# Three groups of gate products per token tile instead of four in a two-layer hybrid trunk kernel

## The chip, the cores and the metric

The kernel runs on one core of a Trainium2 chip. The metric is the device time of one execution in microseconds (us); lower is better.

## The reference

The reference is a trunk of two layers over 1024 tokens of width 1024, in float32. Each layer projects its input, runs four token mixers (forgetting attention, retention, the gated recurrence `hgrn2`, attention on a memory), merges them through per-channel sigmoid gates, and goes through a grouped mixture of experts. Two parts matter here: the recurrence over chunks of 64 tokens, and the gated merge of the four branches.

```python
# gated recurrence, one chunk (q, k, v, log f); b = cumsum(log f)
a = einsum('bhik,bhjk,bhijk->bhij', qn, kn, decay)
o = einsum('bhij,bhjv->bhiv', a, vn) + einsum('bhik,bhkv->bhiv', qn * exp(b), state)
new_state = exp(b_last)[..., None] * state + einsum('bhjk,bhjv->bhkv', kn * exp(b_last - b), vn)
o = o * rsqrt(mean(o * o) + eps) * norm_g * silu(g)
...
# gated merge
up = einsum('bsnc,ncd->bsnd', branches, w_branch[l])
gates = sigmoid(gate.reshape(B, S, 4, 1024))      # gate = x @ w_in[l][:, gate columns]
mixed = sum(gates * up, axis=2) @ w_out[l]
```

## The kernel before

**Numbers.** Every float32 operand of a big product is held as two float16 parts, a high and a low one, and one product is three matmuls (high by high, high by low, low by high) of 128x128 by 128x512. ScalarE (ACT) makes the high part of a chunk of weights (`high_parts`, L785), and VectorE (DVE) the low part from it (`low_parts`, with `low_part` at L1274).

**Units and groups.** The gate columns of the four branches are cut into 16 units of 256 columns; unit `u` is one load of weights into one of two slots. A unit has four groups `g` (two blocks of 128 columns by two halves of 512 tokens), so a layer has 64 groups. `gate(g)` gives the place of the group: `place = g // 16`, which branch is merged, in `ORDER = (0, 1, 3, 2)`; the recurrence's branch is last. In its plain form a group (`gate_group`) is 8 products for the gate into a bank of PA and 2 products for the branch into a bank of PB: 30 matmuls, 120 for the unit. ACT takes the tanh (`gate_tanh`, L979), DVE multiplies (`gate_mul`, L1536), and from place 1 on adds to the running sum as well (L1539).

**The seven-product form.** For the last units of a layer (`sev_group`) the gate product of a unit, seen as 2x2 blocks (input half by column block by token half), is made with seven block products in place of eight. A block product is 4 products, 12 matmuls; the 24 matmuls of the branches stay. This takes sums of weight blocks (`sums_1_3`, `sum_2`, `sum_4`) and sums of blocks of the input (`x_sum_full`, `x_sum_high`, `x_sum_low`; eight pieces per layer). `PLAIN = 9` units are plain and `SEV = 7` are in the seven-product form; `SEV_G = 4 * PLAIN` is the first group of these.

**The order of the work.** It is written out by hand, one program per engine, and every engine runs its own in order. The plain groups are interleaved with the recurrence, tile by tile (128 tokens, `NT = 8`): two groups ahead (`PRE = 2`), four in each tile `t` (`g = PRE + 4 * t` to `g + 3`), two behind the loop, then the seven-product units. In tile `t` TensorE (PE) runs:

1. six transposes into PC (L2418), group `g`, the state product, the running sums of tile `t + 1` into PC, group `g + 1`;
2. the scores (L2441), group `g + 2`, the outputs (L2449, L2454; they post `h_o`);
3. two transposes of the finished output of tile `t - 1` into PC (L2218, `transpose_o`), group `g + 3`.

After `h_o` ACT squares the output (L1096), DVE reduces it (L1689), GpSimd takes the power (L687), and DVE finishes the row into `ON` (L1695 to L1699, posts `h_on`). The two transposed blocks of tile `t - 1` are copied out of PC by ACT (`copy_ot`, L898) and DVE (`low_ot`, L1274 as OT<-PC,OT), which posts `ot_cp`; on DVE `low_ot` stands behind the reduction. The next tile's transposes write the same PSUM tile PC and begin with these waits:

```python
pe.wait_ge(h_pr, at(h_pr, t + 1))
pe.wait_ge(ot_cp, at(ot_cp, 3 * NT + max(t, 1)))
```

With the count as it is posted, the second one waits in tile `t` (from 2 on) for the copy of exactly the blocks that tile `t - 1` transposed in its step 3. In tiles 3, 5 and 7 DVE also makes two pieces of the input sums (L1593 to L1597 and the low part at L1274), and ACT their high parts (L1010).

**Splitting the next unit's weights.** `next_unit_high(g)` and `next_unit_low(g)` stand behind the tanh and the multiplication of group `g`. Which chunks they split depends on `g % 4` alone:

```python
return (range(0), range(0, 3), range(3, 5), range(0))[g % 4]
```

The third of the three chunks at remainder 1 can be made by ACT only when DVE has taken the first.

Of the kernel before, what the change touches and what calls it, by code (L numbers as in the profile page):

```python
# [30 lines left out]
NT = T // P  # L31
# [56 lines left out]
PRE = 2  # L88
ORDER = (0, 1, 3, 2)


PLAIN = 9
SEV_U, SEV_G, SEV = GATE_U + PLAIN, 4 * PLAIN, GATES - PLAIN
RAW = 5
B11, T1, T3, B22, B21, T2, T4, BRANCH = range(8)
# [4 lines left out]
def chunks_to(u):  # L100
    return 8 * min(u, GATE_U) + 5 * min(max(u - GATE_U, 0), PLAIN) + 8 * max(u - SEV_U, 0)

# [19 lines left out]
def trunk(nc, x, mem, w_in, b_in, w_mem_kv, hgrn_lb, hgrn_norm_g, w_branch, w_out, ln_g, ln_b,  # L122
          w_router, b_router, w_e_in, w_e_out, consts, chunk_mask, out):
    with ExitStack() as ctx:
# [315 lines left out]
        def gate(g):  # L440
            u, i = GATE_U + g // 4, g % 4
            c, half = (i // 2, i % 2) if g < SEV_G else QUARTERS[i]
            return u, g // 16, ORDER[g // 16], g // 4 % 4 * 2 + c, c, half
# [329 lines left out]
        def _(act):  # L773
# [58 lines left out]
            with act.Fori(0, LAYERS) as l:  # L832
# [142 lines left out]
                def gate_tanh(g):  # L975
                    u, place, n, d, c, half = gate(g)
                    act.wait_ge(g_z, at(g_z, g + 1))
                    act.wait_ge(g_mul, at(g_mul, g + 1))
                    nc.scalar.activation(TH[g % 2], PA[:, g % 2, :], ACT.Tanh,  # L979
                                         bias=bT[:, 6 + n * KD + d:7 + n * KD + d], scale=0.5 * UN).then_inc(g_sig, 1)  # L980
                    if place == NBR - 1:
                        act.wait_ge(mix_f, at(mix_f, g - 48 + 1))
                        nc.scalar.activation(MIXS[:, d, half, 0, :], MIXF, ACT.Copy, scale=0.5 * UN * SX
                                             ).then_inc(mix_hi, 1)
# [15 lines left out]
                def next_unit_high(g):  # L1000

                    u = GATE_U + g // 4 + 1
                    if u == SEV_U:
                        sev_high(u, (range(0), range(0, 2), range(2, 5), range(5, 8))[g % 4])
                    elif g < SEV_G:
                        high_parts(at, u, next_chunks(g))
# [70 lines left out]
                gate_tanh(1)  # L1077
                next_unit_high(1)
                for t in range(NT):
                    g = PRE + 4 * t  # L1080
                    act.wait_ge(h_tr, at(h_tr, t + 1))
                    nc.scalar.copy(WK[:, 1024:1792], flat(PC, 768)).then_inc(h_tc, 1)
                    if t + 1 < NT:
                        lf_high(t + 1)
                    gate_tanh(g)
                    next_unit_high(g)
                    if t + 1 < NT:
                        decays(t + 1)
                    gate_tanh(g + 1)
                    next_unit_high(g + 1)  # L1090
                    if t in (3, 5, 7):
                        x_sum_high(t // 2 - 1, 0)
                    gate_tanh(g + 2)
                    next_unit_high(g + 2)
                    act.wait_ge(h_o, at(h_o, t + 1))
                    nc.scalar.activation(paired(WK[:, 2560:2816]), by_bank(PD, HD, P), ACT.Square).then_inc(h_sq, 1)  # L1096
                    if t in (3, 5, 7):
                        x_sum_high(t // 2 - 1, 1)
                    if t >= 1:
                        copy_ot(3 * NT + t - 1, 2, t - 1)  # L1100
                    gate_tanh(g + 3)
                    next_unit_high(g + 3)
                for g in range(PRE + 4 * NT, SEV_G):
                    if g == PRE + 4 * NT + 1:
                        copy_ot(4 * NT - 1, 2, NT - 1)
                    gate_tanh(g)
                    next_unit_high(g)
# [154 lines left out]
        def _(v):  # L1262
# [51 lines left out]
            with v.Fori(0, LAYERS) as l:  # L1314
# [215 lines left out]
                def gate_mul(g):  # L1530
                    u, place, n, d, c, half = gate(g)
                    v.wait_ge(g_sig, at(g_sig, g + 3))
                    v.wait_ge(g_mm, at(g_mm, g + 1))
                    acc, up = MIX[:, d, half, :], PB[:, g % 2, :]
                    ups = UPS0 if place == NBR - 1 else UPS[g % 2]
                    stt(acc if place == 0 else ups, TH[g % 2] if g < SEV_G else TH7[g % 4], 1.0, up, ALU.add, ALU.mult).then_inc(g_mul, 1)  # L1536
                    v.drain()
                    if place in (1, 2):
                        tt(acc, acc, ups, ALU.add)  # L1539
                    if place == NBR - 1:  # L1540
                        tt(MIXF7[g % 2], acc, ups, ALU.add).then_inc(mix_f, 1)
# [111 lines left out]
                next_unit_low(1)  # L1653
                for t in range(NT):
                    a, b = t % 2, (t + 1) % 2
                    g = PRE + 4 * t
                    if t + 1 < NT:
                        lf_low(t + 1)
                    gate_mul(g)
                    next_unit_low(g)  # L1660

                    v.wait_ge(h_kv, at(h_kv, t + 1))
                    v.sem_inc(passed, 1)
                    kv = PD[:, :, 0:2 * HD].rearrange("p c (j d) -> p c j d", j=2)
                    tt(hstate[:, a, 1, :, :], hstate[:, a, 0, :, :], over(hdec[:, t % 2, :, 0], HD), ALU.mult)
                    v.drain()
                    tt(hstate[:, a, 1, :, :], hstate[:, a, 1, :, :], kv[:, 0, :, :], ALU.add)
                    v.drain()
                    tt(hstate[:, b, 0, :, :], hstate[:, a, 1, :, :], over(hdec[:, t % 2, :, 1], HD), ALU.mult)
                    v.drain()  # L1670
                    tt(hstate[:, b, 0, :, :], hstate[:, b, 0, :, :], kv[:, 1, :, :], ALU.add).then_inc(h_st, 1)
                    if t + 1 < NT:
                        decayed(t + 1)
                    if t in (3, 5, 7):
                        x_sum_full(t // 2 - 1, 0)
                    gate_mul(g + 1)
                    next_unit_low(g + 1)
                    v.wait_ge(h_a, at(h_a, t + 1))
                    v.sem_inc(passed, 1)
                    nc.vector.copy_predicated(paired(AT),  # L1680
                                              hmask[:, :].unsqueeze(1).unsqueeze(1).to_broadcast([P, 2, 2, P]),
                                              by_bank(PD, P, P)).then_inc(h_am, 1)
                    if t in (3, 5, 7):
                        x_sum_low(t // 2 - 1, 0)
                        x_sum_full(t // 2 - 1, 1)
                    gate_mul(g + 2)
                    next_unit_low(g + 2)
                    v.wait_ge(h_sq, at(h_sq, t + 1))
                    nc.vector.tensor_reduce(st[:, 4:8], heads(SQH), AX.X, ALU.add)  # L1689
                    v.drain()  # L1690
                    ts(st[:, 4:8], st[:, 4:8], 1.0 / HD, GN_EPS, ALU.mult, ALU.add).then_inc(h_var, 1)  # L1691
                    if t >= 1:
                        low_ot(3 * NT + t - 1, 2, t - 1)
                    v.wait_ge(h_rstd, at(h_rstd, t + 1))
                    tt(paired(N1), by_bank(PD, HD, P), over4(st[:, 8:12]), ALU.mult)  # L1695
                    v.drain()
                    tt(heads(N1), heads(N1), ngain[:, :].unsqueeze(1).to_broadcast([P, H, HD]), ALU.mult)
                    v.drain()
                    tt(ON[:, t % 2, :], N1, HN[:, t, 3 * BW:4 * BW], ALU.mult).then_inc(h_on, 1)  # L1699
                    gate_mul(g + 3)  # L1700
                    next_unit_low(g + 3)
                    if t in (3, 5, 7):
                        x_sum_low(t // 2 - 1, 1)
                for g in range(PRE + 4 * NT, SEV_G):
                    if g == PRE + 4 * NT + 1:
                        low_ot(4 * NT - 1, 2, NT - 1)
                    gate_mul(g)
                    next_unit_low(g)
                    if g == PRE + 4 * NT:
                        x_sum_full(3, 0)  # L1710
                x_sum_low(3, 0)
                x_sum_full(3, 1)
# [298 lines left out]
        def _(pe):  # L2011
# [72 lines left out]
            with pe.Fori(0, LAYERS) as l:  # L2084
# [324 lines left out]
                gate_group(1)  # L2409
                for t in range(NT):  # L2410
                    val = HN[:, t, BW:2 * BW]
                    g = PRE + 4 * t
                    pe.wait_ge(h_pr, at(h_pr, t + 1))

                    pe.wait_ge(ot_cp, at(ot_cp, 3 * NT + max(t, 1)))
# [42 lines left out]
                    if t >= 1:  # L2458
                        if t + 1 < NT:
                            pe.wait_ge(h_e, at(h_e, t + 2))  # L2460
                        transpose_o(3 * NT + t - 1, ON[:, (t - 1) % 2, :], 2)
                    gate_group(g + 3)
                for g in range(PRE + 4 * NT, SEV_G):
                    if g == PRE + 4 * NT + 1:
                        pe.wait_ge(h_on, at(h_on, NT))
                        transpose_o(4 * NT - 1, ON[:, (NT - 1) % 2, :], 2)
                    gate_group(g)
# [266 lines left out]
```

## Time and profile before

| what | value |
|---|---|
| time before, median of 3 runs | 2755.81 us (2753.03 to 2756.02) |
| the profiled execution's own time | 2761.64 us |
| its span | 2760.0 us |
| TensorE busy | 2571.6 us, 93% of the span |
| VectorE busy | 1672.1 us, 61% |
| ScalarE busy | 1215.6 us, 44% |
| mean granted TensorE clock | 0.966 of 2.4 GHz |

The span runs from the first to the last instruction; the own time lies 1.6 us above it, and the median 5.8 us below the own time. In the profile a time stamp is in microseconds from the start of the span, "L2332" is a line of the kernel, and an idle time is followed by what ended it. A matmul of 128x512 is recorded with 0.38 us, but the starts of two in a row lie 0.216 us apart, since they overlap; it is the distance of starts that counts in a sum.

### The profile page before, as it was taken

What the parts mean: (1) busy time and instruction counts of PE and PEld (TensorE: products, weight loads), DVE (VectorE), ACT (ScalarE), POOL (GpSimd) and SP (SyncE); (2) the same over time, 40 slices, a digit from 0 to 9 for tenths busy, and PEclk for the clock granted to TensorE, in tenths of its full rate; (3) what the DMA queues carried; (4) which work ended last, traced back from release to release, by engine and by line L of the source; (5) the groups of instructions that cost most, each with busy time, mean ns of one, the idle gap of its engine ahead of it and who ended that gap; (6) DMA issues with size and microseconds to landing.
All of it is one profiled execution on the core that took longest, in us unless ns stands there. A gap on an engine that the chain in (4) does not pass through costs nothing.

```text
span 2760.0 us, 55929 instructions
## 1 busy us (share of the span) xinstructions
PE 2571.6 (93%) x20734; PEld 1588.2 (58%) x20735; DVE 1672.1 (61%) x2735; ACT 1215.6 (44%) x1978; POOL 336.1 (12%) x242
## 2 busy tenths in 40 slices
PE   7999999999999869999979999999999997699993
PEld 5555555554444458888645565555544444688882
DVE  4244574566666658875643455745666666687884
ACT  4245423232343137765642454233323431376774
POOL 0000000000000013443320000000000000144443
PEclk9999999999999979999979999999999998899996
DMA  7210001111115459998843000011111154599996
GB/s 287 78 61 1 32 20 55 42 39 45 51 58 205 153 197 346 363 355 269 250 157 108 32 1 32 21 57 39 39 58 53 53 196 171 196 354 356 362 337 182
DMA packets 153278, 394.15 MB, mean 143 GB/s; under 512 B 14284, under 2 KB 63864, under 8 KB 151872
## 3 DMA queue, kind: packets, MB, share of 16 engines
q1 hardware_dynamic: 135936, 339.09, 34.0%
q0 software_dynamic: 16544, 46.00, 6.8%
q10 hardware_dynamic: 608, 6.55, 0.6%
q8 instruction: 116, 1.90, 0.3%
q14 instruction: 74, 0.61, 0.1%
HBM read 342.41 MB, written 53.38 MB: 143 GB/s over the span
## 4 chain that ended last, share of the span: by engine, by line
PE 80%; issue 5%; DVE 5%; DMA 3%; PEld 3%; ACT 2%; DVEq 1%; SPq 0%; PEldq 0%; POOL 0%; ACTq 0%; POOLq 0%
PE PA L2567 12%; PE PA L2021 7%; PE PA L2022 7%; PE PA L2023 7%; PE PD L2575 6%; PE PB L2567 4%; PE PA L2332 4%; PE PC L2016 3%; PE PB L2023 3%; PE PB L2022 3%; PE PB L2021 3%; PE PD L2332 2%; PE PC L2332 2%; PE PD L2021 2%; PE PD L2022 2%
## 5 line engine op out<-in xcount | busy, mean ns | idle before, releaser
L2567 PE MATMUL PA<-RC,XT 128*128 128x160 f16 x4752 | 424.1, 234 | 9.3 <-DVE XT L1274 8.1
L2567 PEld LDWEIGHTS PA<-RC,XT 128*128 128x128 f16 x4752 | 348.3, 98 | 17.3 <-DVE XT L1274 9.1
L1274 DVE SCALAR_TENSOR_TENSOR W<-W 128x512 f16<-128x512 f32 (+2 forms) x362 | 228.6, 663 | 147.1 <-ACT W L785 126.4
L1274 DVE SCALAR_TENSOR_TENSOR XT<-OT,XT 128x1024 f16<-128x1024 f32 x256 | 294.3, 1216 | 2.0 <-ACT XT L1148 2.0
L2021 PE MATMUL PA<-XT,W 128*128 128x512 f16 x768 | 292.3, 381 | 0.8 <-issue 0.7
L2022 PE MATMUL PA<-XT,W 128*128 128x512 f16 x768 | 291.8, 380 | 0.0
L2023 PE MATMUL PA<-XT,W 128*128 128x512 f16 x768 | 291.8, 380 | 0.0
L1148 ACT ACTIVATE XT<-OT 128x1024 f16<-128x1024 f32 x240 | 230.3, 1051 | 1.5 <-issue 1.5
L2567 PE MATMUL PB<-RC,XT 128*128 128x160 f16 x1584 | 197.3, 234 | 0.0
L2575 PE MATMUL PD<-W,WK 128*128 128x512 f16 x792 | 186.7, 386 | 6.7 <-ACT WK L1179 6.3
L785 ACT ACTIVATE W<-W 128x512 f16<-128x512 f32 (+2 forms) x250 | 140.7, 597 | 102.4 <-DVE W L1274 57.7
L979 ACT ACTIVATE WK<-PA,bT 128x512 f32<-128x512 f32 x72 | 49.5, 688 | 286.9 <-PE PA L2023 286.9
L687 POOL TENSOR_TENSOR st<-st,CO 128x4 f32<-128x4 f32 x16 | 16.2, 1013 | 1222.7 <-DVE st L1691 1222.7
L1274 DVE SCALAR_TENSOR_TENSOR W<-RA,W 128x1024 f16<-128x1024 f32 x128 | 148.0, 1216 | 11.7 <-ACT W L1154 11.4
L2021 PE MATMUL PA<-W,XT 128*128 128x512 f16 (+1 forms) x384 | 133.0, 346 | 7.7 <-DVE ZF L1327 5.6
L2022 PE MATMUL PA<-W,XT 128*128 128x512 f16 (+1 forms) x384 | 132.8, 346 | 0.0
L2023 PE MATMUL PA<-W,XT 128*128 128x512 f16 (+1 forms) x384 | 132.7, 346 | 0.0
L2575 PEld LDWEIGHTS PD<-W,WK 128*128 128x128 f16 x792 | 75.8, 99 | 96.2 <-issue 13.1
L2023 PEld LDWEIGHTS PA<-XT,W 128*128 128x128 f16 x768 | 75.3, 98 | 91.3 <-issue 1.1
L2567 PEld LDWEIGHTS PB<-RC,XT 128*128 128x128 f16 x1584 | 125.8, 98 | 0.0
L2021 PEld LDWEIGHTS PA<-XT,W 128*128 128x128 f16 x768 | 75.2, 98 | 86.7 <-issue 3.1
L1536 DVE SCALAR_TENSOR_TENSOR MKV<-WK,PB 128x512 f32<-128x512 f32 x96 | 65.7, 684 | 95.6 <-PE PB L2023 91.9
(410 smaller groups left out, 4997.3 us busy)
## 6 DMA issues: line engine op xcount, KB each, us to landing
OT<-in_w_e_in_dram SPq DMA_DIRECT2D x256, 512.0 KB, 10.9
RA<-in_w_e_out_dram SPq DMA_DIRECT2D x128, 512.0 KB, 11.2
W<-in_w_in_dram SPq DMA_DIRECT2D x104, 512.0 KB, 4.7
W<-in_w_branch_dram SPq DMA_DIRECT2D x32, 256.0 KB, 4.9
W<-in_w_out_dram SPq DMA_DIRECT2D x16, 512.0 KB, 5.4
x_rows<-RC SPq DMA_DIRECT2D x16, 512.0 KB, 5.8
y_sum<-RC SPq DMA_DIRECT2D x16, 512.0 KB, 6.6
OT<-y_sum SPq DMA_DIRECT2D x16, 512.0 KB, 4.8
```

What stands on the lines that cost most here:

```text
L785: nc.scalar.activation(WS[slot][:, k, 0, 0:n], W[slot][:, k + SPARE, 0:n], ACT.Copy, scale=SW).then_inc(w_hi, 1)
L979: nc.scalar.activation(TH[g % 2], PA[:, g % 2, :], ACT.Tanh, bias=bT[:, 6 + n * KD + d:7 + n * KD + d], scale=0.5 * UN).then_inc(g_sig, 1)
L1148: nc.scalar.activation(EIS[:, 0, k, :], WEI[:, k, :], ACT.Copy, scale=SW).then_inc(ei_hi, 1)
L1274: return stt(dst, src, scale, high, ALU.mult, ALU.subtract)
L1536: stt(acc if place == 0 else ups, TH[g % 2] if g < SEV_G else TH7[g % 4], 1.0, up, ALU.add, ALU.mult).then_inc(g_mul, 1)
L2016: q = nc.tensor.transpose(flat(dst)[:, k * P:(k + 1) * P], src[:, k * P:(k + 1) * P], ident)
L2021: mm(dst, lhs(0), rhs(0), start=first, stop=False)
L2022: mm(dst, lhs(0), rhs(1), start=False, stop=False)
L2023: return mm(dst, lhs(1), rhs(0), start=False, stop=last)
L2332: q = mm(dst, WS[u % 2][:, SLOT_OF[b], i, k * P:(k + 1) * P], x(j, k), start=first and k + i + j == 0, stop=last and k == 3 and i == 1, sk ...
L2567: q = mm(dst, EIS[:, s, k, n * P:(n + 1) * P], of[:, x, k, :], start=k == 0 and b < 3 and s + x == 0, stop=k == KD - 1 and s == 1, skip_gr ...
L2575: q = mm(PD[:, half, :], of[:, a, k, 0:RM], EOS[:, b, k, half * HALF:(half + 1) * HALF], start=k == 0 and a + b == 0, stop=k == KF - 1 and ...
```

## The change

`PLAIN` goes from 9 to 7, and each tile of the recurrence has three groups (`STEP = 3`) instead of four. Units 7 and 8 of each layer, which were plain, are in the seven-product form, 9 of 16 units in place of 7. The fourth group of a tile, which stood behind `transpose_o` on PE and behind the recurrence's output on ACT and DVE, is gone from all three programs. No wait is changed.

```diff
-PLAIN = 9
+PLAIN = 7
+STEP = 3
 SEV_U, SEV_G, SEV = GATE_U + PLAIN, 4 * PLAIN, GATES - PLAIN
...
 (each of ACT, DVE and PE)
                 for t in range(NT):
-                    g = PRE + 4 * t
+                    g = PRE + STEP * t
...
 (ACT)
                         copy_ot(3 * NT + t - 1, 2, t - 1)
-                    gate_tanh(g + 3)
-                    next_unit_high(g + 3)
-                for g in range(PRE + 4 * NT, SEV_G):
+                for g in range(PRE + STEP * NT, SEV_G):
...
 (DVE)
                     tt(ON[:, t % 2, :], N1, HN[:, t, 3 * BW:4 * BW], ALU.mult).then_inc(h_on, 1)
-                    gate_mul(g + 3)
-                    next_unit_low(g + 3)
                     if t in (3, 5, 7):
                         x_sum_low(t // 2 - 1, 1)
...
 (PE)
                         transpose_o(3 * NT + t - 1, ON[:, (t - 1) % 2, :], 2)
-                    gate_group(g + 3)
-                for g in range(PRE + 4 * NT, SEV_G):
+                for g in range(PRE + STEP * NT, SEV_G):
```

The places behind the loop that name `PRE + 4 * NT` name `PRE + STEP * NT` likewise.

## Rows read from the trace of the kernel before

**Rows 1.** The page: span, and busy time by engine.
```profile
span 2760.0 us, 55929 instructions
...
PE 2571.6 (93%) x20734; PEld 1588.2 (58%) x20735; DVE 1672.1 (61%) x2735; ACT 1215.6 (44%) x1978; POOL 336.1 (12%) x242
```

**Rows 2.** Busy time by stretch, layer 0: recurrence with plain groups; seven-product units.
```profile
430.00:690.00 260.00, 260.00 (x1569) 130.99 (x1568) 143.98 (x253) 76.68 (x140) 8.11 (x8) 1.00 0.14 43
704.00:850.00 146.00, 146.00 (x678) 66.21 (x677) 97.64 (x152) 64.13 (x109) 0.00 (x0) 1.00 0.19 60
```

**Rows 3.** Waits from 420 to 700 us: engine, line, waited for, total, times, longest.
```profile
ACT WK L979 <- PE PA L2023: 143.4, 36, 6.5
```

**Rows 4.** Chain that ended last: one block product of the seven-product form.
```profile
705.22 2.59 PE PA L2332 x12
```

**Rows 5.** Timeline of PE around the end of tile 3: start, us.
```profile
545.37 0.38 PE L2023 MATMUL PB<-OT,W 128*128 128x512 f16 x1
...
546.52 0.47 PE L2454 MATMUL PD<-hstate,WK 64*64 64x64 f32 x16
546.92 0.44 PE L2218 MATMUL PC<-CO,ON 128*128 128x128 f32 x2
547.20 0.38 PE L2021 MATMUL PA<-XT,W 128*128 128x512 f16 x1
```

**Rows 6.** Timeline of PE, tile 1, the two transposes.
```profile
486.55 0.44 PE L2218 MATMUL PC<-CO,ON 128*128 128x128 f32 x2
```

**Rows 7.** Timeline of DVE, end of tile 1.
```profile
485.48 0.69 DVE L1536 SCALAR_TENSOR_TENSOR RA<-WK,PB 128x512 f32<-128x512 f32 x1 [5.61 <-PE PB L2023]
487.12 0.42 DVE L1689 TENSOR_REDUCE st<-WK 128x4 f32<-128x256 f32 x1 [0.95 <-ACT WK L1096]
...
487.73 0.42 DVE L1274 SCALAR_TENSOR_TENSOR OT<-PC,OT 128x256 f16<-128x256 f32 x1
...
489.93 0.43 DVE L1699 TENSOR_TENSOR ON<-WK,RC 128x256 f32<-128x256 f32 x1
```

**Rows 8.** Timeline of ACT, end of tile 1.
```profile
487.02 0.38 ACT L898 ACTIVATE OT<-PC 128x256 f16<-128x256 f32 x1
```

**Rows 9.** Timeline of DVE, tile 5.
```profile
592.65 1.28 DVE L1274 SCALAR_TENSOR_TENSOR W<-W 128x512 f16<-128x512 f32 x2
...
600.40 0.68 DVE L1536 SCALAR_TENSOR_TENSOR MKV<-WK,PB 128x512 f32<-128x512 f32 x1
...
607.44 0.68 DVE L1536 SCALAR_TENSOR_TENSOR MKV<-WK,PB 128x512 f32<-128x512 f32 x1
...
609.42 0.42 DVE L1274 SCALAR_TENSOR_TENSOR OT<-PC,OT 128x256 f16<-128x256 f32 x1
```

**Rows 10.** Timeline of ACT: end of tile 3, and the third chunk in tile 5.
```profile
548.30 0.38 ACT L898 ACTIVATE OT<-PC 128x256 f16<-128x256 f32 x1
...
586.24 0.63 ACT L785 ACTIVATE W<-W 128x512 f16<-128x512 f32 x1 [1.67 <-DVE W L1274]
```

**Rows 11.** Timelines of ACT and PE at the first seven-product unit.
```profile
692.98 0.58 ACT L1034 COPY PA<-PC 128x512 f32<-128x512 f32 x1
...
693.61 2.76 PE L2332 MATMUL PA<-RC,W 128*128 128x512 f16 x12 [1.44 <-ACT PA L1034]
```

**Rows 12.** Timeline of PE: three idle times elsewhere in the kernel.
```profile
867.22 0.39 PE L2021 MATMUL PA<-W,RA 128*128 128x512 f16 x1 [1.91 <-DVE W L1274]
...
1514.89 0.39 PE L2021 MATMUL PD<-W,XT 128*128 128x512 f16 x1 [2.09 <-DVE RA L1336]
...
2242.08 0.39 PE L2021 MATMUL PA<-W,RA 128*128 128x512 f16 x1 [2.04 <-DVE W L1274]
```

**Rows 13.** Busy time by stretch, PE first, PEclk behind POOL: what followed such idle times.
```profile
867.20:870.40 3.20, 3.18 (x15) 1.49 (x16) 0.00 (x0) 0.54 (x1) 0.00 (x0) 1.00 1.02 417
1515.90:1519.10 3.20, 3.20 (x10) 1.29 (x9) 0.08 (x1) 0.76 (x3) 0.00 (x0) 0.50 0.03 10
...
2242.90:2246.10 3.20, 3.20 (x9) 1.06 (x8) 0.00 (x0) 0.00 (x0) 0.00 (x0) 0.50 1.02 410
```

More of the change, by code:

```diff
@@ L1100, in _ @@
                         copy_ot(3 * NT + t - 1, 2, t - 1)
-                    gate_tanh(g + 3)
-                    next_unit_high(g + 3)
-                for g in range(PRE + 4 * NT, SEV_G):
-                    if g == PRE + 4 * NT + 1:
+                for g in range(PRE + STEP * NT, SEV_G):
+                    if g == PRE + STEP * NT + 1:
                         copy_ot(4 * NT - 1, 2, NT - 1)
@@ L1655, in _ @@
                     a, b = t % 2, (t + 1) % 2
-                    g = PRE + 4 * t
+                    g = PRE + STEP * t
                     if t + 1 < NT:
@@ L1699, in _ @@
                     tt(ON[:, t % 2, :], N1, HN[:, t, 3 * BW:4 * BW], ALU.mult).then_inc(h_on, 1)
-                    gate_mul(g + 3)
-                    next_unit_low(g + 3)
                     if t in (3, 5, 7):
                         x_sum_low(t // 2 - 1, 1)
-                for g in range(PRE + 4 * NT, SEV_G):
-                    if g == PRE + 4 * NT + 1:
+                for g in range(PRE + STEP * NT, SEV_G):
+                    if g == PRE + STEP * NT + 1:
                         low_ot(4 * NT - 1, 2, NT - 1)
@@ L1708, in _ @@
                     next_unit_low(g)
-                    if g == PRE + 4 * NT:
+                    if g == PRE + STEP * NT:
                         x_sum_full(3, 0)
@@ L2411, in _ @@
                     val = HN[:, t, BW:2 * BW]
-                    g = PRE + 4 * t
+                    g = PRE + STEP * t
                     pe.wait_ge(h_pr, at(h_pr, t + 1))
@@ L2461, in _ @@
                         transpose_o(3 * NT + t - 1, ON[:, (t - 1) % 2, :], 2)
-                    gate_group(g + 3)
-                for g in range(PRE + 4 * NT, SEV_G):
-                    if g == PRE + 4 * NT + 1:
+                for g in range(PRE + STEP * NT, SEV_G):
+                    if g == PRE + STEP * NT + 1:
                         pe.wait_ge(h_on, at(h_on, NT))
```

## The prediction, made before the changed kernel was run

> **What bounds the kernel now.** I read the page first: TensorE is busy for 93% of the span, the next engine for 61% [rows 1]. Busy time by stretch then says where the change lies. From 430 to 690 us, where layer 0 runs the recurrence with the plain groups, TensorE is busy for 260.0 of 260.0 us at the full clock of 2.4 GHz, and in the seven-product units from 704 to 850 us for 146.0 of 146.0 [rows 2]. DVE has 144 and 98 us of work there. The view of waits agrees: it is ACT's tanh that waits for PE, 143.4 us in 36 waits [rows 3]. So in this stage the time is TensorE's list of matmuls, and two things can happen: a shorter list gives its time back at once, and any wait that nothing covers any more is paid at once. The profile of before can't show the second kind as idle time, since the groups cover it. I looked for it in the code, going through the waits that stand behind the group to be removed, and then in the timelines of the three engines.
>
> **The gain.** A block product of twelve matmuls takes 2.59 us on the chain [rows 4], 0.216 us each. A plain unit is 4 x 30 = 120 matmuls, 25.9 us; one in seven-product form 84 + 24 = 108, 23.3 us, and the stretch of rows 2 shows no idle time in such units. Each converted unit gives 2.59 us, four units (two per layer) 10.4 us. The two units add weight sums and splits on DVE and ACT, four sums and three more chunks each; DVE is busy 98 of 146 us in that stretch [rows 2], so TensorE covers them and I cost them at nothing. Were they not covered, four sums and three splits at about 0.64 us (two splits took 1.28 us [rows 9]) would be 4.5 us per unit, 18 us in all. The DMAs are the same number, triggered by the same counts of finished groups, and I cost them at nothing too: a unit is loaded a whole unit ahead.
>
> **The wait that loses its cover.** With group g + 3 gone, PE goes from `transpose_o` straight to the next tile's transposes. These wait for `ot_cp`, the copy of what `transpose_o` has just written. Before, 6.5 us of matmuls (30 x 0.216) lay between; now nothing. Behind this wait PE's whole queue stands: the transposes, the next group, and ACT and DVE behind them. Tiles 1 to 6 are followed by such a wait (tile 0 writes no such block, tile 7 has no successor), six per layer. Its length is the end of `low_ot` less the time at which PE is free:
>
> - *Tile 1.* The two transposes start at 486.55 [rows 6]; 0.28 us later the next matmul could start, as 546.92 to 547.20 in tile 3 shows [rows 5], so PE is free at 486.83. `low_ot` starts at 487.73 and takes 0.42 [rows 7]: 488.15. With 0.05 for the hand-over (ACT's copy ends at 693.56, PE starts at 693.61 [rows 11]) the wait is 1.35 us. Tile 4 has the same order and the same 1.35.
> - *What the tiles differ in.* Splits hang on g % 4. Before, group g + 2 of every tile had remainder 0, with no splits between its multiplication and the reduction. With three groups per tile the pattern wanders: g + 2 has remainder 0, 3, 2, 1, 0, 3, 2, 1 in tiles 0 to 7. DVE takes these splits ahead of the reduction and of `low_ot`.
> - *Tile 2* (remainder 2): the multiplication ends at 486.17 in tile 1's times, two splits (1.28, with 0.17 ahead) bring DVE to 487.6, and the reduction, which began at 487.12, slides by 0.5: 1.85 us.
> - *Tile 6* (remainder 2, place 1): the multiplication is followed by the sum into the accumulator, as long again (0.69 us [rows 7]), and the slide is 1.0: 2.35 us.
> - *Tile 3* (remainder 1): three splits, and the third must go DVE to ACT to DVE; in tile 5 ACT stood 1.67 us for that [rows 10]. The branch product ends at 545.37 + 0.38 = 545.75 [rows 5], multiplication to 546.5, first split to 547.3, ACT's third high part to 548.0. Only then come ACT's square, the high part of an input sum (about 1 us) and `copy_ot`, at 549.2 instead of 548.30 [rows 10]; `low_ot` ends at 550.05. PE is free at 547.20 [rows 5]: 2.9 us.
> - *Tile 5* is the worst. Groups g and g + 1 now have three and two splits, where there were two and none. DVE had no idle time from the state update to group g + 2: the multiplications of g + 1 and g + 2 start at 600.40 and 607.44 right behind input sums [rows 9]. One more split with its round over ACT moves the first by 0.95 us, two splits of 1.28 move the second by 2.3. `low_ot` goes from 609.42 [rows 9] to 611.7, ends at 612.15, and PE is free at 607.57: 4.6 us.
>
> The sum is 1.35 + 1.85 + 2.9 + 1.35 + 4.6 + 2.35 = 14.4 us per layer.
>
> **The other waits of the stage.** `h_on` (ahead of the state product) came 2.2 us after `low_ot` (490.36 against 488.15 [rows 7]) and has the transposes and a group, 7.5 us, as cover: nothing. If that cover were gone too, it would be 2.2 us a tile. `h_pr` and `h_st` are done within group g + 1: nothing. After tile 7 the weight sums of the first seven-product unit now stand ahead of the reduction, so `h_on` of tile 7 comes about 0.3 us after PE wants it. At the first seven-product unit PE already waits for ACT's copy (the row says 1.44 us; counted from the twelfth start it is 1.6) [rows 11]. DVE's list up to there is the same less one multiplication and its idle time, PE's is a group shorter, and following both lists I get 2.3 us: 0.7 more. So 1.0 us per layer, 15.4 with the above, 30.8 for both layers (the second layer runs the same lists). Net of the gain: +20.4 us.
>
> **The clock.** After idle times of 2.09 and 2.04 us in otherwise dense work the granted clock fell to 0.50, that is 1.2 GHz, for the stretches 1515.9 to 1519.1 and 2242.9 to 2246.1; after one of 1.91 us it stayed at 1.00 [rows 12, 13]. Matmul starts were twice as far apart there (10 and 9 in 3.2 us against 15), so such a stretch, 3.2 us and a little at its ends, costs half of its length, 1.7 us. The changed kernel has per layer two idle times clearly longer than those (2.9, 4.6) and two just above (2.35, and 2.3, behind which a second wait would absorb part). I charge the long ones in full and the others by half: 1.7 + 1.7 + 0.85 + 0.35 = 4.6 us per layer, 9.2 in all. From below the cost is 0 (the clock ignores them), from above all eight, 13.6 us. In the words of the Trainium skill (TensorE: Matmul & The Clock Gate, What's actually happening), "the default state is throttled, and activity releases the throttle". Taken alone that makes each of the eight idle times a candidate, and the sum by it would be 20.4 + 13.6 = +34 us.
>
> **Sum.** 30.8 + 9.2 - 10.4 = +29.6 us. On the profiled execution's own time of 2761.6 us that is 2791.2; the median lies 5.8 us lower, which gives 2785.4 us.
>
> **The rivals.**
>
> *The waits come, the clock holds.* The idle times are single and short beside 20 us of dense matmuls, and the 1.91 us one was ignored [rows 12, 13]. Against it stand the two that were not. +20.4 us: 2776.
>
> *Every idle time costs clock, or DVE trails further in tiles 3, 5 and 7.* DVE is without idle time there already [rows 9], and each delay of it falls on PE. +34 to +40 us: 2790 to 2796.
>
> *The wait is in truth covered, and the kernel is faster.* This needs `low_ot` to be done when PE arrives. It would be so if the copy ran ahead of the reduction on DVE: ACT's copy starts at 487.02 [rows 8], 0.7 us before DVE takes it. But the order on DVE is fixed, and the copy can't start before PE's transposes have ended at 486.99. With only the 1.0 us per layer of the transition left: 2.0 - 10.4 = -8.4 us, 2747. The point from which it decides: the waits would have to sum to less than 4.2 us per layer, an average of 0.7 where the shortest that I find is 1.35.
>
> *No change that can be measured.* Waits of 3 to 7 us per layer without loss of clock, 2750 to 2761. It needs DVE to be much less late in tiles 3 and 5 than its list says.
>
> **How the numbers follow.** Change of at least 0.2% is about what a measurement of this kernel can tell, 5.5 us. Chances: my forecast 0.5, the held clock 0.3, the dear case 0.12, no change 0.04, faster 0.04. So slower 0.92, same 0.04, faster 0.04. The range of 8 in 10 takes in the two large cases, with the lengths of the waits uncertain by some 20% (6 us) below the held clock, and the lower part of the dear case: 2769 to 2794. The likeliest case's own range is 2779 to 2793.
>
> **What would show it.** The changed kernel's timeline of PE has six idle times per layer ahead of L2418, none ahead of the first two tiles, ended by DVE's `low_ot`, the longest after tile 5 (about 4.6 us) and then after tile 3, about 1.35 after tiles 1 and 4; the stage's idle PE time grows by some 15 us per layer. In the seven-product stretch L2332 has 1.29 times its matmuls, 23.3 us per unit and no new idle time. The granted clock shows halves of a few us behind tiles 3 and 5. Wrong would be: idle times ended by POOL or `h_on` (then it is the recurrence's own chain), a dense recurrence stage, or new idle times within the seven-product units.

## The result and the profile after

The changed kernel takes 2791.81 us (median of 4 runs, 2789.95 to 2799.16) against 2754.74 us for the kernel before: +37.1 us, a ratio of 1.0139 with a 95% interval of 1.0122 to 1.0156. Slower was forecast, with 2785.4 us; the time lies inside the stated range of 2769 to 2794, 7.5 us more above before than the forecast had it. Ratios and their intervals are given as they were recorded; the quotient of the two medians beside them can differ by up to 0.0006 (here it is 1.0135).

The first lines of the page of after: TensorE has the same busy time as before in a span that is 28.3 us longer [rows 1].

```profile
span 2788.3 us, 55975 instructions
...
PE 2572.7 (92%) x20686; PEld 1587.9 (57%) x20687; DVE 1694.7 (61%) x2771; ACT 1229.6 (44%) x2002; POOL 333.2 (12%) x242
```

That busy time did not fall, with 48 matmuls fewer, is a first hint at the clock: matmuls at 1.2 GHz are recorded longer, as the transposes below show.

The waits of PE in the stage of layer 1, from 1815 to 2090 us of after (line, who was waited for, total, times, longest):

```profile
PE PC L2415 <- DVE OT L1273: 13.4, 6, 4.2
PE PA L2329 <- ACT PA L1035: 2.1, 1, 2.1
PE PA L2329 <- ACT WK L1047: 0.9, 1, 0.9
```

Before, this view of either layer holds only the two small lines of the seven-product unit (1.4 and 0.9 us; [rows 11] has the first). Now there are six waits for DVE's `low_ot` (L1273, OT), the lines of the code having moved by a few. One by one in layer 0, in the timeline of PE (start, length, line, what, count, and in brackets the idle time ahead and what ended it; the transposes that post the block stand ahead of the first and of the fifth):

```profile
481.13 0.44 PE L2215 MATMUL PC<-CO,ON 128*128 128x128 f32 x2
482.87 1.43 PE L2415 MATMUL PC<-CO,WK 128*128 128x128 f32 x6 [1.31 <-DVE OT L1273]
...
510.09 1.39 PE L2415 MATMUL PC<-CO,WK 128*128 128x128 f32 x6 [1.63 <-DVE OT L1273]
...
538.50 1.51 PE L2415 MATMUL PC<-CO,WK 128*128 128x128 f32 x6 [2.80 <-DVE OT L1273]
...
566.53 0.87 PE L2415 MATMUL PC<-CO,WK 128*128 128x128 f32 x6 [1.22 <-DVE OT L1273]
...
590.02 0.44 PE L2215 MATMUL PC<-CO,ON 128*128 128x128 f32 x2
594.71 1.51 PE L2415 MATMUL PC<-CO,WK 128*128 128x128 f32 x6 [4.25 <-DVE OT L1273]
...
622.90 1.54 PE L2415 MATMUL PC<-CO,WK 128*128 128x128 f32 x6 [2.17 <-DVE OT L1273]
```

The reader is to see three things. The waits stand after tiles 1 to 6, and one of the six runs of transposes, behind tile 4, took 0.87 us and the other five 1.39 to 1.54: the same work at the full and at half clock. The bracket counts from the recorded end of the transposes, 0.44 us after their start, while the next matmul could start after 0.28 us; so each wait is 0.16 us longer than its bracket, 1.46 after tile 1 (482.87 less 481.41) and 4.41 after tile 5.

The clock, by stretches behind these waits in layer 0 (first two lines) and in layer 1 of after (columns: PE, PEld, DVE, ACT, POOL busy, then PEclk, DMA, GB/s):

```profile
483.00:486.20 3.20, 3.20 (x11) 1.79 (x11) 1.70 (x4) 1.11 (x2) 0.47 (x1) 0.50 0.84 283
...
592.30:598.90 6.60, 4.19 (x13) 2.34 (x14) 4.84 (x10) 2.43 (x4) 1.01 (x1) 0.50 0.34 114
...
1872.80:1876.00 3.20, 3.20 (x18) 1.81 (x19) 1.69 (x4) 1.12 (x2) 0.54 (x1) 1.00 0.85 290
...
1925.10:1928.30 3.20, 3.20 (x19) 1.77 (x20) 2.75 (x5) 1.11 (x2) 0.22 (x1) 1.00 0.00 0
1978.40:1981.40 3.00, 3.00 (x11) 1.83 (x12) 2.31 (x4) 1.11 (x2) 0.51 (x1) 0.50 0.03 5
```

In layer 0 the clock was halved behind five of the six waits, behind those after tiles 3 and 5 for twice as long; in layer 1 behind two, after tiles 5 and 6.

The stage as a whole, from the first running sums over the first seven-product part to the first output product. Rows of PE's timeline, before:

```profile
425.96 0.82 PE L2398 MATMUL PC<-WK,CO 128*128 128x256 f16 x6
...
686.83 0.38 PE L2332 MATMUL PC<-XT,W 128*128 128x512 f16 x1
...
854.77 0.39 PE L2021 MATMUL PA<-W,RA 128*128 128x512 f16 x1 [1.92 <-DVE W L1274]
```

and after:

```profile
426.97 0.82 PE L2395 MATMUL PC<-WK,CO 128*128 128x256 f16 x6
...
660.92 0.81 PE L2329 MATMUL PC<-XT,W 128*128 128x512 f16 x3
...
876.14 0.39 PE L2018 MATMUL PA<-W,RA 128*128 128x512 f16 x1 [1.92 <-DVE W L1273]
```

The same three marks were read in every traced kernel. They give this table, in us, layer 0 / layer 1 (the kernels below the second row are those of the experiments):

| kernel | recurrence | seven-product units | both |
|---|---|---|---|
| before | 260.9 / 260.9 | 167.9 / 168.0 | 428.8 / 428.8 |
| after | 234.0 / 226.8 | 215.2 / 215.2 | 449.2 / 442.0 |
| early transposes | 210.8 / 210.8 | 215.2 / 215.8 | 426.0 / 426.6 |
| cover only | 282.0 / 285.9 | 165.7 / 165.7 | 447.6 / 451.6 |
| keep busy | 223.9 / 223.9 | 215.2 / 215.2 | 439.1 / 439.1 |
| splits behind | 227.0 / 226.4 | 215.6 / 215.6 | 442.6 / 442.1 |
| copies first | 220.4 / 220.3 | 216.9 / 216.9 | 437.4 / 437.2 |
| early, and copy first | 210.8 / 210.8 | 213.2 / 213.2 | 424.0 / 424.0 |
| early in before | 260.9 / 260.8 | 167.9 / 168.0 | 428.8 / 428.8 |
| again (the changed kernel once more) | 229.5 / 226.8 | 215.2 / 215.2 | 444.8 / 442.1 |

All of the loss is in this stage: 20.4 in layer 0 and 13.2 in layer 1, 33.5 us unrounded, in after's trace, where the spans differ by 28.3. The rest of the kernel was 5 us shorter than in the traced execution of before, which with 2761.64 us lay 6.9 us above the median given here.

### The profile page after: what moved, and what is told of

Read it like the earlier page. It is cut to its first block, busy times and chain, and to the rows that moved or that the text cites. A ratio compares the mean times of both kernels' runs of the same rounds, so it can differ in the third digit from the quotient of the medians.

```text
span 2788.3 us, 55975 instructions
## 1 busy us (share of the span) xinstructions
PE 2572.7 (92%) x20686; PEld 1587.9 (57%) x20687; DVE 1694.7 (61%) x2771; ACT 1229.6 (44%) x2002; POOL 333.2 (12%) x242
## 3 DMA queue, kind: packets, MB, share of 16 engines
q1 hardware_dynamic: 135936, 339.09, 33.5%
## 4 chain that ended last, share of the span: by engine, by line
PE 46%; issue 44%; DVE 4%; DMA 3%; ACT 1%; DVEq 1%; POOL 1%; SPq 0%; ACTq 0%; POOLq 0%
PE PA L2563 12%; PE PD L2571 6%; PE PA L2329 5%; PE PB L2563 4%; PE PD L2329 3%; PE PC L2329 3%; PE PB L2020 2%; PE PB L2018 2%; PE PB L2019 2%; PE PC L2013 2%; PE PB L2578 2%; PE PA L2018 1%; PE PA L2019 1%; PE PA L2020 1%; DMA y_sum<-WK,BR 1%
## 5 line engine op out<-in xcount | busy, mean ns | idle before, releaser
L1273 DVE SCALAR_TENSOR_TENSOR W<-W 128x512 f16<-128x512 f32 (+2 forms) x374 | 236.8, 664 | 146.1 <-ACT W L786 123.6
L1273 DVE SCALAR_TENSOR_TENSOR XT<-OT,XT 128x1024 f16<-128x1024 f32 x256 | 294.3, 1216 | 1.3 <-ACT XT L1147 1.3
L2018 PE MATMUL PA<-XT,W 128*128 128x512 f16 x640 | 247.4, 387 | 1.0 <-issue 1.0
L2019 PE MATMUL PA<-XT,W 128*128 128x512 f16 x640 | 246.5, 385 | 0.0
L2020 PE MATMUL PA<-XT,W 128*128 128x512 f16 x640 | 245.6, 384 | 0.0
L786 ACT ACTIVATE W<-W 128x512 f16<-128x512 f32 (+2 forms) x230 | 129.1, 594 | 95.1 <-DVE W L1273 52.7
L1273 DVE SCALAR_TENSOR_TENSOR W<-RA,W 128x1024 f16<-128x1024 f32 x128 | 148.0, 1216 | 11.7 <-ACT W L1153 11.4
L980 ACT ACTIVATE WK<-PA,bT 128x512 f32<-128x512 f32 x56 | 38.5, 687 | 234.4 <-PE PA L2020 234.4
L691 POOL DMA_INDIRECT RC<-x_rows,BR x33 | 36.7, 1111 | 736.4 <-DVE BR L1855 706.2
L1153 ACT ACTIVATE W<-RA 128x1024 f16<-128x1024 f32 x120 | 116.9, 1055 | 3.9 <-PE PB L2578 3.9
```

What stands on the lines that cost most here:

```text
L786: nc.scalar.activation(WS[slot][:, k, 0, 0:n], W[slot][:, k + SPARE, 0:n], ACT.Copy, scale=SW).then_inc(w_hi, 1)
L1153: nc.scalar.activation(EOS[:, 0, k, :], WEO[:, k, :], ACT.Copy, scale=SW).then_inc(eo_hi, 1)
L1273: return stt(dst, src, scale, high, ALU.mult, ALU.subtract)
L2018: mm(dst, lhs(0), rhs(0), start=first, stop=False)
L2019: mm(dst, lhs(0), rhs(1), start=False, stop=False)
L2020: return mm(dst, lhs(1), rhs(0), start=False, stop=last)
```

## The experiments

The kernel before took 2760.88 us beside the first four experiments and 2754.87 us beside the others, so kernels are compared by their ratio to it. My theory after the result was that of the prediction: the block copy that PE has to wait for, plus the clock that the idle time costs, less the gain of the seven-product form, which arrives in full. Its rivals: the recurrence's own chain or VectorE bounds the stage with three groups per tile; the two more seven-product units cost something themselves; the clock has another cause.

**Early transposes.** PE transposes the output of tile `t - 1` ahead of group `g + 2`; ACT and DVE copy it there.

```diff
 (PE)
                     q.then_inc(h_a, 1)
+                    if t >= 1:
+                        if t + 1 < NT:
+                            pe.wait_ge(h_e, at(h_e, t + 2))
+                        transpose_o(3 * NT + t - 1, ON[:, (t - 1) % 2, :], 2)
                     gate_group(g + 2)
...
                     q.then_inc(h_o, 1)
-                    if t >= 1:
-                        if t + 1 < NT:
-                            pe.wait_ge(h_e, at(h_e, t + 2))
-                        transpose_o(3 * NT + t - 1, ON[:, (t - 1) % 2, :], 2)
 (ACT: copy_ot from behind the square to ahead of gate_tanh(g + 2);
  DVE: low_ot from behind the reduction to behind copy_predicated)
```

> All of the change, but the two transposes of tile t-1 and their copies on ACT and DVE stand ahead of group g+2 instead of behind the outputs, so that the copy of a block lies under a group of matmuls. The output is the reference's. My theory (the exposed wait for that copy, and the clock it costs, are the loss; the gain of the seven-product form arrives in full): no idle time ahead of the tile's six transposes, no new stretch at half clock in the recurrence stage, idle time at the first seven-product unit as in the changed kernel (about 3 us per layer, 0.7 more than before). Time 10.4 us less than before, plus about 2 us: 2746 us, faster than before by 0.3%. Rival (the stage is bound by the recurrence's own chain or by VectorE once there are three groups per tile): the idle time turns up at another wait (h_on, h_am) and the time stays above 2770 us.

Measured: ratio 0.9986 (0.9977 to 0.9995), 2757.80 us against 2760.88 on its chip. PE's waits from 420 to 860 us:

```profile
PE PA L2329 <- ACT PA L1035: 2.1, 1, 2.1
PE PA L2018 <- DVE W L1273: 1.9, 1, 1.9
PE PC L2395 <- DVE WK L1273: 0.9, 1, 0.9
PE PA L2329 <- ACT WK L1047: 0.9, 1, 0.9
PE PC L2215 <- DVE ON L1698: 0.2, 1, 0.2
```

The six waits are gone, and nothing of their size has come in their place; the view of before has the 1.9 us line too. New are 0.9 us for the running sums made in tile 6, where DVE is late, and 0.2 us for `h_on` ahead of the last transposes. The recurrence took 210.8 us in both layers, so the chain of the recurrence fits into three groups per tile. Against before the kernel gained 3.9 us where 8.4 were expected: the stage gained 2.8 us in layer 0 and 2.2 in layer 1, where I had 4.2 by the sum 5.2 less 1.0. The two new waits, 1.1 us, account for most of the 1.4 us that are missing in layer 0. The 0.6 us between the layers go with a half clock behind the 2.1 us wait at the first seven-product unit of layer 1:

```profile
2019.00:2022.20 3.20, 3.20 (x9) 1.15 (x8) 3.05 (x3) 0.00 (x0) 0.00 (x0) 0.50 0.00 0
```

**Cover only.** `PLAIN = 9` with `STEP = 3`: the groups are out of the tiles, but no unit is converted.

```diff
-PLAIN = 7
+PLAIN = 9
 STEP = 3
```

> Three groups per tile, but nine plain units as before: the groups taken out of the tiles run behind the loop, and no unit changes its form. The output is the reference's. My theory: the six waits per layer are the same as in the changed kernel (1.3, 1.6, 2.8, 1.2, 4.3, 2.2 us, 13.4 per layer), with the half-clock stretches that go with them (8 to 15 us of time in all), while the 2.3 us per layer at the first seven-product unit vanish since the input sums are ready. Time 2755 + 27 - 5 + 12 = 2789 us, range 2783 to 2797; the matmuls of 10.4 us more than in the changed kernel are offset in part by those 5 to 6 us. Rival (the loss lies in the two more seven-product units): within 0.3% of before.

Measured: ratio 1.0141 (1.0125 to 1.0156), 2798.29 us against 2760.88: +37 to +39 us. The forecast of 2789 us was made on 2755 us, so it was +34 us, with a range of +28 to +42. PE's waits from 420 to 860 us:

```profile
PE PC L2415 <- DVE OT L1273: 13.4, 6, 4.2
PE PA L2329 <- ACT WK L1047: 0.2, 1, 0.2
```

The same six waits to the tenth, with nine plain units. So they come from the removed cover and not from the seven-product form. The waits at the first seven-product unit all but vanished, as expected. In this trace the clock was halved behind three of the six waits in layer 0 and behind all six in layer 1, where the recurrence took 3.9 us more than in layer 0.

**Keep busy.** The changed kernel with extra matmuls where PE waits; their results are overwritten.

```diff
                         transpose_o(3 * NT + t - 1, ON[:, (t - 1) % 2, :], 2)
+                        if t + 1 < NT:
+                            pe.wait_ge(g_sig, at(g_sig, g + 4))
+                            for i in range((6, 8, 13, 6, 20, 10)[t - 1]):
+                                mm(PA[:, (g + 3) % 2, :], XS[:, 0, 0, 0:P], XS[:, 0, i % KD, 0:HALF], start=True, stop=True)
```

> The changed kernel with 6, 8, 13, 6, 20, 10 extra matmuls of 128x512 (0.216 us each, on loaded data, into the PA bank that the next group starts afresh) behind the two transposes of tiles 2 to 7's predecessors, so that TensorE is busy while it waits for the copy. The output is the reference's. It takes the clock apart from the wait: the wait's length stays, the idle time goes. Theory (the loss of clock is caused by the idle time): no half-clock stretch in the recurrence stage of either layer; time 2755 + 27 + 2 - 10.4 = 2774 us, range 2769 to 2780, that is some 15 us under the changed kernel. Rival (the clock falls there for another cause, or costs nothing because VectorE sets the pace): time within 4 us of the changed kernel's 2791.

Measured: ratio 1.0079 (1.0064 to 1.0095), 2781.12 us against 2760.88. The stretches of the recurrence in the two layers:

```profile
426.00:648.00 222.00, 221.98 (x1387) 112.67 (x1386) 124.22 (x227) 65.64 (x124) 8.10 (x8) 1.00 0.12 36
...
1807.00:2031.00 224.00, 223.98 (x1404) 113.90 (x1403) 125.61 (x229) 66.95 (x125) 8.09 (x8) 1.00 0.12 36
```

against those of after:

```profile
426.00:660.00 234.00, 220.62 (x1341) 112.58 (x1339) 124.87 (x228) 66.77 (x125) 8.11 (x8) 0.95 0.11 35
...
1816.00:2043.00 227.00, 213.62 (x1342) 109.82 (x1341) 125.04 (x229) 66.96 (x125) 8.10 (x8) 0.98 0.12 36
```

Idle time became work, and the granted clock was 1.00 throughout. The stage has the same length in both layers, 439.1 us, 10.3 more than before: this is the price of the waits less the gain, without any clock. What after has above it in its trace, 10.1 us in layer 0 and 2.9 in layer 1, is the clock. More matmuls made the kernel faster than the changed one: +0.8% over before in place of +1.4%.

**Splits behind.** The splits of the third group stand behind the output's work on DVE and behind the block copy on ACT.

```diff
                     gate_mul(g + 2)
-                    next_unit_low(g + 2)
...
                     tt(ON[:, t % 2, :], N1, HN[:, t, 3 * BW:4 * BW], ALU.mult).then_inc(h_on, 1)
+                    next_unit_low(g + 2)
 (ACT likewise: next_unit_high(g + 2) behind copy_ot)
```

> The changed kernel, but the splits that belong to a tile's third group stand behind the recurrence's output on VectorE and behind the copy on ScalarE, as they did for the fourth group. The output is the reference's. Theory (the length of a wait follows from where the splits fall by g % 4): the waits after tiles 2 and 6 become those of tiles 1 and 4 (1.3 us), the one after tile 3 falls from 2.8 to 2.0, the one after tile 5 stays at 4.2 since its splits belong to the first two groups; 11.4 us per layer in place of 13.4, time 4 us less than the changed kernel plus or minus what the clock does. Rival (the length is set by the recurrence's chain h_o, square, reduction alone): the waits stay as they are.

Measured: ratio 1.0096 (1.0081 to 1.0112), 2786.39 us against 2760.88. Four of the waits in the timeline of PE, after tiles 2, 3, 5 and 6:

```profile
507.10 0.87 PE L2415 MATMUL PC<-CO,WK 128*128 128x128 f32 x6 [1.22 <-DVE OT L1273]
...
532.95 1.51 PE L2415 MATMUL PC<-CO,WK 128*128 128x128 f32 x6 [1.93 <-DVE OT L1273]
...
589.45 1.51 PE L2415 MATMUL PC<-CO,WK 128*128 128x128 f32 x6 [4.25 <-DVE OT L1273]
...
616.85 0.87 PE L2415 MATMUL PC<-CO,WK 128*128 128x128 f32 x6 [1.22 <-DVE OT L1273]
```

1.63 and 2.17 became 1.22, 2.80 became 1.93, and 4.25 stayed, each as the place of the splits says. The sum is 11.1 us per layer in place of 13.4. The time fell by more than the 4 us expected: the ratio went from 1.0139 to 1.0096, some 12 us, of which the shorter waits are 4.5. The stage's traces differ by 6.6 us in layer 0 and by nothing in layer 1 (442.0 and 442.1), so what the other executions gained beyond the waits is not shown.

**Copies first.** On top of that, ACT copies the block ahead of the square, and DVE ahead of the reduction.

```diff
 (DVE)
+                    if t >= 1:
+                        low_ot(3 * NT + t - 1, 2, t - 1)
                     v.wait_ge(h_sq, at(h_sq, t + 1))
 (ACT: copy_ot ahead of the wait for h_o)
```

> The changed kernel with the splits of the third group behind (as in the fourth experiment) and the copies of the transposed blocks taken by ScalarE ahead of the square and by VectorE ahead of the reduction. PE's order stays. The output is the reference's. Theory: the wait then holds the two copies alone, 0.38 and 0.42 us with their hand-overs: 1.0 us after tiles 1, 2, 4 and 6, 1.1 after tile 3, and 3.7 after tile 5, where VectorE is late: 8.8 us per layer in place of 11.2, some 5 us less than the fourth experiment; it stays slower than before by 0.6 to 0.9%. Rival (any copy placed first hides the wait): below 0.5 us each, and the time at or under that of before.

Measured: ratio 1.0058 (1.0043 to 1.0074), 2772.32 us against 2754.87. PE's waits from 420 to 860 us:

```profile
PE PC L2415 <- DVE OT L1273: 8.5, 6, 3.6
PE PA L2329 <- ACT PA L1035: 3.2, 1, 3.2
```

The waits sum to 8.5 us per layer (expected 8.8), five of them between 0.93 and 1.02, the one after tile 5 still 3.64. So about 1 us was left with both copies put first: what they take with their hand-overs. Of the orders tried, only another place on PE's list hid it. The first seven-product unit waited 3.2 us, 1.1 more than in after; that its work on DVE now starts later is my reading and was not tested. Some 10 us fell against the fourth experiment where 5 were expected; the stage's traces fell by 10.1 us in both layers together, 5.3 of it in the waits, and the clock was halved behind two waits per layer in place of three.

**Early, and copy first.** The early transposes, and at the first seven-product unit ACT's copy ahead of the last split and input sum.

```diff
+                sev_high(SEV_U, range(5, 7))
+                act.wait_ge(sev_mm, at(sev_mm, 1))
+                nc.scalar.copy(sev_banks(0)[2], sev_banks(0)[0]).then_inc(sev_cp, 1)
+                sev_high(SEV_U, range(7, 8))
                 x_sum_high(3, 0)
...
                     nc.scalar.copy(P16, six).then_inc(sev_cp, 1)
+                    if w == 0:
+                        x_sum_high(3, 1)
 (both taken out of their old places)
```

> The changed kernel with the early transposes of the first experiment, and with ScalarE's copy for the first seven-product unit taken ahead of the split and the input sum it stood behind, the other input sum taken behind the second copy. The output is the reference's. Theory: the 2.1 us of idle time at that unit fall to 0.3, the 0.9 us behind it may grow by 0.4, so 1.4 us per layer less than with the early transposes alone: ratio to before 0.9976 against 0.9986 (2.8 us less). Rival (VectorE's input sums set the time there, in whatever order ScalarE copies): no more than with the early transposes, 0.9986.

Measured: ratio 0.9964 (0.9950 to 0.9978), 2745.47 us against 2754.87, the fastest version of all: 9.9 us less than before, of which the trace has 4.8 per layer in this stage. PE's waits from 420 to 850 us:

```profile
PE PA L2335 <- DVE WK L1630: 0.9, 1, 0.9
PE PC L2401 <- DVE WK L1279: 0.9, 1, 0.9
PE PC L2221 <- DVE ON L1704: 0.2, 1, 0.2
```

The stage gained 2.0 us per layer on the early transposes alone (2.6 in layer 1, where that trace had lost clock), where 1.4 were expected. The rival, VectorE as the limit there, fell.

**Early in before.** The early transposes in the kernel before.

> The kernel before, with only the early transposes and their copies: four groups per tile, nine plain units. The output is the reference's. Theory: there the copy had a group as its cover already, so that nothing is gained: within 0.1% of before, and what the first experiment gained on before belongs to the seven-product form. Rival (the early place is better in itself): faster by 3 us or more, and the two more seven-product units bring nothing.

Measured: ratio 1.0000 (0.9991 to 1.0009), 2754.81 us against 2754.87, and the stage is 428.8 us as before. With four groups per tile the copy was covered, and its early place is worth nothing by itself. So the early transposes' gain on before is that of the two more seven-product units.

**Again.** The changed kernel once more, for another trace.

> The changed kernel itself, once more. The waits are fixed by the order of the work, so their lengths repeat to 0.1 us in both layers. For the granted clock: if the length of an idle time decided whether the clock falls, the same waits would be followed by it as in the first trace (after tiles 1, 2, 3, 5 and 6 in layer 0, after 5 and 6 in layer 1). I expect another selection, with 5 to 15 us of time lost, and executions of the same kernel that differ by some us for that.

Measured: 2788.85 us. Stretches behind the waits after tiles 1, 3, 4 and 5 of layer 0:

```profile
482.10:485.30 3.20, 3.20 (x18) 1.85 (x19) 1.68 (x4) 1.11 (x2) 0.59 (x1) 1.00 0.86 292
...
534.40:537.60 3.20, 3.20 (x18) 1.81 (x19) 2.74 (x5) 1.11 (x2) 0.26 (x1) 1.00 0.00 0
559.90:563.10 3.20, 3.20 (x12) 1.48 (x10) 1.70 (x4) 1.11 (x2) 0.25 (x1) 0.50 0.02 5
587.20:593.80 6.60, 4.46 (x14) 2.48 (x15) 4.57 (x10) 2.15 (x4) 1.01 (x1) 0.50 0.28 94
```

The waits repeat within 0.01 us, the clock does not: behind tile 1 (1.31 us) and tile 3 (2.79 us) it held this time, and behind tile 4 (1.22 us) it fell. Behind tiles 5 and 6 it fell in both layers of both traces. So the length of an idle time alone does not decide whether the clock falls. Above the 439.1 us of the keep-busy kernel the stage had 5.7 us in layer 0 and 3.0 in layer 1, 8.7 in all, against 13.0 in the first trace.

## Why the prediction was right

**The gain.** Forecast 2.59 us per unit. Two more units lengthen the seven-product stretch by 47.3 us, 23.3 each and 0.65 for the longer wait at the first. They added no idle time beyond that, so the added sums and splits lay under PE's work, as costed. The control with the early transposes in before shows that the early kernel's gain is theirs.

**The wait.** Forecast six per layer, ended by `low_ot`, with 1.35, 1.85, 2.9, 1.35, 4.6 and 2.35 us, 14.4 in all. Counted in the same way they measured 1.46, 1.79, 2.96, 1.38, 4.41 and 2.33, 14.3 in all. That the splits' place, by the remainder of g % 4, makes the waits after tiles 2, 3 and 6 longer was tested alone and held. In tile 6 my terms, 0.5 us and a sum of 0.69, make a slide of 1.2 us where I wrote 1.0; measured were 0.95 (2.33 less tile 4's 1.38), so that number came out better than its working.

**The other waits.** For `h_on` after tile 7 0.3 us were forecast and none came. At the first seven-product unit 0.7 us more were forecast and 0.65 came. Net of the gain the two layers were to cost 20.4 us; the keep-busy kernel, which has the waits and not the loss of clock, had 20.6 in its trace and 1.0079 as its ratio, 21.8 us.

**The clock.** This is the term that was mis-sized. I took from two rows of before that idle times above 2.0 us cost clock and shorter ones do not, and charged 9.2 us. The two traces had 13.0 and 8.7. The size of the sum was about right, but the rule behind it was not, so that part of the agreement is luck: waits of 1.2 to 1.6 us were followed by half clock in some executions, and waits of 2.8 us were not in others. The price of one stretch held better: the counts that I gave for it, 10 and 9 starts against 15, are no factor of two, but in the timeline of before the starts in the second stretch, from 2243.10 us on, lie 0.43 us apart against 0.216.

The median of the changed kernel lies 37.1 us above before. Less the waits and the gain, 20.6 to 21.8 us, this leaves some 15 to 17 us in the executions that were not traced; the first traced one was the shortest of its four, and the second, a single one, shorter still. That this is the clock of the stage is worked out from times only and not shown in a trace. Outside the stage the two traces of the changed kernel took 1897.1 and 1900.3 us, 1.6 and 4.8 more than a median execution of before would if its stage took the traced 857.6; so some of the 2 to 8 us above the traced 13.0 and 8.7 may lie there.

My bound from above, eight stretches of 1.7 us and so 13.6, was too low. The changed kernel has seven idle times above 1 us per layer (six waits and the 2.1 us at the first seven-product unit), and I had counted four, and behind the longest ones the clock was halved for two stretches' worth. The trace of the cover-only kernel, with the same six waits, shows it: its recurrence took 282.0 and 285.9 us, where 260.9 and the waits of 14.3 make 275.2, so some 17 us went beyond the waits.

The keep-busy kernel had a granted clock of 1.00, with matmuls in place of the idle time. This agrees with the sentence of the Trainium skill that I quoted (TensorE: Matmul & The Clock Gate, What's actually happening), that activity releases the throttle. I had applied that sentence to eight idle times only, which gave the same 13.6 us as my own bound; each of the fourteen was a candidate.

**The rivals.** The covered wait (faster) failed by the 14.3 us of waits per layer; it is what the early transposes make true. The dear case, at +34 to +40 us, is where the median came to lie. I gave it 0.12, for a mechanism that was in part the right one, more clock lost than the long idle times alone, and in part not, since DVE did not trail further than forecast. The held clock, given 0.3, happened in neither trace.

## What to carry to other kernels

Work that is taken out of a hand-written order is also a cover: before removing it, list each wait that stood behind it on its engine, and the position on the other engines of what ends that wait. Here a saving of 5.2 us per layer uncovered waits of 14.3, and moving one small step ahead of a remaining group brought it back. When a pattern by `g % 4` meets a loop whose step changes from 4 to 3, work that always fell in the same place starts to wander, and its worst place sets a price of its own. Short idle times in a dense stage should be priced with the clock that they may cost, as a range and not by a threshold.

## What the runs showed of the hardware that was not expected

- Idle times of 1.2 to 1.6 us between stretches of dense matmuls were followed, in some executions, by more than 3 us at 1.2 GHz, and with matmuls in their place the clock held; the same idle time, in the same place of the same kernel, cost nothing in another (1.31 us after tile 1: 0.50 in one trace, 1.00 in the next; 2.80 us after tile 3 of layer 0: 0.50 and 1.00).
- Filling 14.3 us of waits per layer with 63 matmuls whose results are overwritten made the kernel some 0.6% faster than leaving TensorE idle (ratios 1.0079 and 1.0139 to the kernel before).
- A run of six float32 transposes took 0.84 to 0.88 us at the full clock and 1.5 at the half (less where the clock changed on the way), so that its recorded length alone tells the clock of its moment.
